# Pooling groups in reverse order, their sums on VectorE alone, values between the pooling maps, and no meeting before the prompt attention

## The reference

```python
def causal_multiscale_pool(u_hist, u_new, positions, w_pool, pool_scale):
    ...
    for g, w in enumerate(POOL_WINDOWS):
        sl = slice(g * POOL_GROUP_W, (g + 1) * POOL_GROUP_W)
        wsum = cs[:, end:end + S, sl] - cs[:, end - w:end - w + S, sl]
        count = jnp.minimum(float(w), positions + 1.0)[:, None]
        outs.append(wsum / count - uf[..., sl])
    d = jnp.stack(outs, axis=2)
    y = jnp.einsum('bsgi,gio->bsgo', d, w_pool.astype(jnp.float32)).reshape(B, S, POOL_W)
    y = y * pool_scale.astype(jnp.float32)
...
    pool_out, new_hist = causal_multiscale_pool(u_hist, u, positions, w_pool, pool_scale)
    attn_out = attend(q_nope, q_rope, lat, k_rope, w_uk, w_uv)
    x = x + gate1 * (jnp.concatenate([pool_out, attn_out], axis=-1) @ w_out)
```

## Time and profile before

| | us |
|---|---|
| runs of the kernel before (3) | 1543.78, 1548.8, 1551.41; median 1548.8 |
| the profiled execution's own time | 1546.44 |
| its span, first to last instruction | 1544.6 |
| TensorE busy in the span | 1489.1 (96%) |
| VectorE, ScalarE, GpSimd busy | 681.6, 426.7, 395.4 |

### The profile page before, as it was taken

One profiled execution on the slowest core, in us unless ns is written; L12 is line 12 of the kernel. 1 busy time (PEld: TensorE's weight loads), 2 busy tenths in 40 slices (PEclk: granted clock), 3 DMA queues, 4 the chain that ended last, 5 costly groups with the idle time before them and its releaser, 6 DMA issues.

```text
span 1544.6 us, 23703 instructions
## 1 busy us (share of the span) xinstructions
PE 1489.1 (96%) x9757; PEld 1338.5 (87%) x9757; DVE 681.6 (44%) x1464; ACT 426.7 (28%) x920; POOL 395.4 (26%) x295
## 2 busy tenths in 40 slices
PE   6899878999999999999999999999999999999998
PEld 4799766666676666689999999999999999999997
DVE  3854756566443333366663223232332323323245
ACT  4421445555433333332230110201102021020244
POOL 1232412222331111160233330604206042060400
PEclk8799999999999999999999999999999999999999
DMA  9511132332544444360012120301103021030103
GB/s 347 224 48 57 72 102 79 127 106 87 196 168 164 162 160 155 124 199 14 28 44 66 41 69 1 96 14 54 56 1 96 14 65 45 1 108 3 42 1 116
DMA packets 92442, 137.18 MB, mean 89 GB/s; under 512 B 13707, under 2 KB 64855, under 8 KB 88103
## 3 DMA queue, kind: packets, MB, share of 16 engines
q1 hardware_dynamic: 82229, 93.37, 18.5%
q0 software_dynamic: 5760, 37.75, 6.9%
q10 hardware_dynamic: 4346, 4.54, 0.9%
HBM read 121.98 MB, written 13.79 MB: 88 GB/s over the span
## 4 chain that ended last, share of the span: by engine, by line
PE 88%; DVE 5%; ACT 2%; issue 2%; DMA 2%; POOL 0%; SPq 0%; ACTq 0%; DVEq 0%
PE psa L1242 25%; PE psa L1256 24%; PE psa L1220 6%; PE psa L1092 4%; PE psa L1119 4%; PE psa L787 3%; PE psa L1159 3%; PE psa L832 3%; PE psa L955 3%; PE psa L993 3%; PE psa L1122 2%; DMA wm<-in_w_mod 2%; PE psa L976 1%; PE psa L1143 1%; PE psa L393 1%
## 5 line engine op out<-in xcount | busy, mean ns | idle before, releaser
L1242 PE MATMUL psa<-hhi,wr 128*128 128x384 f32 (+1 forms) x1536 | 374.5, 326 | 0.0
L1242 PEld LDWEIGHTS psa<-hhi,wr 128*128 128x128 f32 x1536 | 270.8, 188 | 0.1
L1256 PE MATMUL psa<-g_hi,wd_hi 128*128 128x384 f32 (+1 forms) x768 | 251.3, 327 | 0.0
L1242 PE MATMUL psa<-hlo,wr 128*128 128x384 f32 (+1 forms) x768 | 250.3, 326 | 0.0
L1256 PE MATMUL psa<-g_hi,wd_lo 128*128 128x384 f32 (+1 forms) x768 | 250.3, 326 | 0.0
L1256 PE MATMUL psa<-g_lo,wd_hi 128*128 128x384 f32 (+1 forms) x768 | 250.2, 326 | 0.0
L1673 ACT ACTIVATE g_relu<-psa 128x384 f32<-128x384 f32 (+1 forms) x96 | 45.4, 473 | 600.9 <-PE psa L1242 600.9
L2155 DVE SCALAR_TENSOR_TENSOR xT<-psa,modT,xT 128x384 f32<-128x384 f32 (+1 forms) x216 | 123.2, 571 | 189.4 <-PE psa L1256 160.6
L566 POOL TENSOR_SCALAR wr<-wraw 128x1024 fp32r<-128x1024 f32 x34 | 36.4, 1070 | 564.1 <-PE psa L1242 491.8
L2222 DVE TENSOR_TENSOR psa<-psa,g_relu 128x384 f32<-128x384 f32 (+1 forms) x96 | 52.2, 544 | 261.3 <-ACT g_relu L1673 261.3
L1242 PEld LDWEIGHTS psa<-hlo,wr 128*128 128x128 f32 x768 | 144.1, 188 | 0.1
(11 more groups left out here) (328 smaller groups left out, 2482.2 us busy)
## 6 DMA issues: line engine op xcount, KB each, us to landing
wmod<-in_w_mod SPq DMA_DIRECT2D x8, 2048.0 KB, 7.9
wraw<-in_w_up SPq DMA_DIRECT2D x32, 512.0 KB, 4.0
wraw<-in_w_down SPq DMA_DIRECT2D x32, 512.0 KB, 3.3
wm<-in_w_mod SPq DMA_DIRECT2D x4, 2048.0 KB, 20.1
x_scr<-xT SPq DMA_DIRECT2D x1, 4352.0 KB, 19.6
wraw<-in_w_out SPq DMA_DIRECT2D x8, 512.0 KB, 6.7
out_y_p<-yst SPq DMA_DIRECT2D x8, 512.0 KB, 2.6
xstage<-in_x_prompt SPq DMA_DIRECT2D x3, 1024.0 KB, 10.8
```

The source lines that it names most:

```text
L1242: mm = pe.matmul(out[:, :N], w[:, c * P:c * P + P], x[:, c, c0:c0 + N], start=(c == 0 and q == 0), stop=(c == KD - 1 and q == 2))
L1256: mm = pe.matmul(out[:, :N], w[:, c, n * P:n * P + P], x[:, c, c0:c0 + N], start=(c == 0 and q == 0), stop=(c == FG - 1 and q == 2))
```

## The change

The groups are multiplied in the order 3, 2, 1, 0 (`GROUP_ORDER`), and the weights loaded in that order. VectorE makes all four groups' sums; GpSimd's are gone, and with them the buffers `pc` and `pd`. The pooling maps run in the order of groups 1, 0, 3, 2 (`MAP_ORDER`). The first two tiles' latents are turned inside the product of the last group, and the rotary key is turned by a plain matmul into one bank's two row strips instead of by a transpose into two banks. The first query tile uses other banks. Value tiles and maps alternate, starting with a value tile; tiles 5, 6 and 7 move behind the turning of the queries and the keys. The meeting of the engines is gone; single waits take its place.

```diff
+GROUP_ORDER = (3, 2, 1, 0)
+MAP_ORDER = (1, 0, 3, 2)
+Q_BANKS = ((5, 6), (0, 1))
...
-    pa = at("pa", [P, PADL + TP], F32, R0)
+    pa = at("pa", [P, PADL + TP], F32, X0 + 20864)
...
         sp.wait_ge(sem("stored"), 16 * (2 + NB))
-        barrier(sp, 1)
+        sp.wait_ge(sem("q_mm"), TT)
+        sp.wait_ge(sem("split"), 10)
...
-        g.wait_ge(sem("u_ev"), NG)
-        g.wait_ge(sem("d_raw"), 1)
-        g.wait_ge(sem("split"), 10)
-        sums = ((pc, pc_s), (pd, pd_s))
...
-            g.tensor_tensor(a[:, first:], have[0][:, first:], have[0][:, first - s:PADL + TP - s], ALU.add)
...
-        barrier(g, 1)
...
+        def turn_rope(t):
+            n = tile_rows(t)
+            out = bank(4)[32 * (t % 2):32 * (t % 2) + DR, 0:n]
+            pe.matmul(out, krot[:n, t, :], ident[:n, :n], start=True, stop=True).then_inc(sem("turned"), 1)
...
+            if m == 3:
+                turn_latents(0)
+                turn_latents(1)
             for c in range(KD):
+                if m == 3 and c == 2:
+                    pe.wait_ge(sem("u_ev"), 3)
+                    turn_rope(0)
+                    turn_rope(1)
...
-            pe.wait_ge(sem("u_ev"), 4 if t else 3)
...
+            if t == 1:
+                pe.wait_ge(sem("u_ev"), 4)
...
-        pool_map(0)
-        for t in range(PT):
-            if t in (3, 6):
-                pool_map(t // 3)
+
+        def make_v(t):
...
-        pool_map(3)
-        barrier(pe, 1)
+
+        make_v(0)
+        for t in range(1, 5):
+            make_v(t)
+            pool_map(t - 1)
...
-            out = bank(3 - w)
+            out = bank(3 - w) if hh else bank(4 + w)
...
+            if hh == 0:
+                pe.wait_ge(sem("pool_ev"), 9)
...
         for w in range(2):
             turn_q(0, w)
+        make_v(5)
+        make_v(6)
         for m in range(2):
             make_k(m)
+        make_v(7)
         scores(0)
...
-        act.wait_ge(sem("d_raw"), 3)
+        for m in range(3):
+            u_out(m)
         turned_hi(0)
         turned_hi(1)
-        act.wait_ge(sem("u_mm"), 12)
+        u_out(3)
         pool_in_hi(0)
...
-        barrier(act, 1)
...
-        for g in range(3):
+        v.wait_ge(sem("wq_split"), 1)
+        for g in GROUP_ORDER[:3]:
             pool_raw(g)
...
         turned_lo(1)
-        pool_in_lo(0)
+        pool_raw(GROUP_ORDER[3])
...
             if t in (1, 4, 7):
-                g = t // 3 + 1
-                if g >= 2:
-                    pool_in_lo(g - 1)
+                pool_in_lo(t // 3)
...
+        values_out(0)
+        values_out(1)
+        pool_in_lo(3)
+        for t in range(2, 5):
+            values_out(t)
...
-        barrier(v, 1)
...
+        v.wait_ge(sem("lat_out"), 64)
         for w in range(2):
             q_lo(0, w)
+        values_out(5)
+        values_out(6)
         for m in range(2):
             k_lo(m)
+        values_out(7)
+        v.memset(pt0[:, 1, 0:P], 0.0)
         rope_lo(0)
```

More of the change, by code:

```diff
@@ L817, in _, with turn_latents @@
             project(t, range(KD))
+        def turn_latents(t):
+            n = tile_rows(t)
+            if t >= 2:
+                pe.wait_ge(sem("turned_lo"), t - 1)
+            pack = bank(2 + t % 2)
+            for c in range(CC):
+                pe.transpose(pack[:, c * P:c * P + n], cqn[:n, t, c * P:c * P + P], ident[:n, :n])
+                pe.transpose(pack[:, (2 + c) * P:(2 + c) * P + n], lat[:n, t, c * P:c * P + P], ident[:n, :n])
+        def turn_rope(t):
+            n = tile_rows(t)
+            out = bank(4)[32 * (t % 2):32 * (t % 2) + DR, 0:n]
+            pe.matmul(out, krot[:n, t, :], ident[:n, :n], start=True, stop=True).then_inc(sem("turned"), 1)
         for m in range(NG):
@@ L835, in _ @@
                             mm.then_inc(sem("u_mm"), 1)
-        def turn_latents(t):
-            n = tile_rows(t)
-            pe.wait_ge(sem("u_ev"), 4 if t else 3)
[L840 to L846, removed]
         def make_q(t):
@@ L869, in _ @@
                 turn_latents(t + 2)
+                turn_rope(t + 2)
         for g in range(NG):
@@ L875, in _, with pool_map @@
         mm.then_inc(sem("hist_back"), 1)
-        def pool_map(g):
-            if g == 0:
+        def pool_map(m):
+            g = MAP_ORDER[m]
+            if m == 0:
                 pe.wait_ge(sem("split"), 10)
@@ L881, in pool_map @@
                 pe.wait_ge(sem("q_ev"), TT)
-            pe.wait_ge(sem("d_lo"), g + 1)
-            if g >= 2:
-                pe.wait_ge(sem("pool_ev"), 3 * (g - 1))
+            pe.wait_ge(sem("d_lo"), m + 1)
+            if m >= 2:
+                pe.wait_ge(sem("pool_ev"), 3 * (m - 1))
             for q, (w, x) in enumerate(products(wg_hi, wg_lo, d_hi, d_lo)):
                 for b, (c0, N) in blocks():
-                    mm = pe.matmul(bank(POOL_BANKS[g % 2][b])[:, :N], w[:, 1, g * P:g * P + P], x[:, g, c0:c0 + N],
+                    mm = pe.matmul(bank(POOL_BANKS[m % 2][b])[:, :N], w[:, 1, g * P:g * P + P], x[:, g, c0:c0 + N],
                                    start=(q == 0), stop=(q == 2))
@@ L904, in _ @@
             mm.then_inc(sem("v_mm"), 1)
-        pool_map(3)
-        barrier(pe, 1)
+        make_v(0)
+        for t in range(1, 5):
+            make_v(t)
+            pool_map(t - 1)
         def turn_q(hh, w):
-            out = bank(3 - w)
+            out = bank(3 - w) if hh else bank(4 + w)
             if w == 0:
                 pe.wait_ge(sem("qh_in"), 16 * hh + 16)
+            if hh == 0:
+                pe.wait_ge(sem("pool_ev"), 9)
+            if hh == 1:
+                pe.wait_ge(sem("v_ev"), PT)
             if w == 0 and hh >= 1:
                 pe.wait_ge(sem("mod_ev"), 3 + hh)
-            if w == 1 and hh == 1:
-                pe.wait_ge(sem("q_lo"), 2)
             if w == 1 and hh >= 2:
@@ L1420, in _, with u_out @@
                     h_high(piece[0], c)
-        for m in range(NG):
+        def u_out(m):
+            g = GROUP_ORDER[m]
             act.wait_ge(sem("u_mm"), 3 * (m + 1))
@@ L1473, in _ @@
         pool_in_hi(3)
-        for g in range(NG):
-            act.wait_ge(sem("pool_mm"), g + 1)
-            if g == 2:
+        for m, g in enumerate(MAP_ORDER):
+            act.wait_ge(sem("pool_mm"), m + 1)
+            if m == 2:
                 act.wait_ge(sem("q_rotated"), TT)
@@ L1509, in first_four @@
                 act.wait_ge(sem("pt_mm"), groups_turned(i) - 1)
+                if i == 4:
+                    act.wait_ge(sem("stored"), 16 * (2 + NB))
                 if t == 4 and hh >= 1:
@@ L1972, in the_rest @@
                 v.wait_ge(sem("pv_mm"), 2 * hh - 1)
+            if i == 4:
+                v.wait_ge(sem("stored"), 16 * (2 + NB))
             if t == 4 and hh >= 1:
```

79 lines of the change are left out of this document (32 added, 47 removed).

## The result

The changed kernel takes 1532.23 us (median of 6 runs, 1530.49 to 1537.52); the kernel before, in the same comparison, 1544.62 (6 runs, 1543.24 to 1551.41). The ratio is 0.9913, 95% interval 0.9896 to 0.9929, so 11 to 16 us less. The profiled execution took 1530.49, the shortest of the six.

A forecast was written before the change was run, and what follows sets the result against it. TensorE was taken as the bound, holding 88% of the chain of waits. 12.0 us at the scores plus 1.5 for the clock gave 13.5, so 1532.9 or 1535.3 by starting figure; forecast 1534, range 1527 to 1541.

The forecast's parts named there:

- the main sum: From the pooling-input product to the prompt attention: first scores at 211.7 instead of 223.66, 12.0 us earlier.
- Sums on VectorE: Pooling-input product: VectorE makes all groups' sums, 9.7 us for window 16, each done before the next group, 12.0 apart.
- The third query tile: Query loop: tile 2 starts at 167.8, 5.1 us earlier, after a pause of 2.0 in place of 5.06, at full clock.
- The key turn: Rotary key by plain matmul: 0.27 us each against 0.11 by transpose, bounds 0.11 and 0.31; five add 0.16 each.
- Values, maps, no meeting: After the queries: value tiles cover the 2.55 pause, the meeting's 1.60 goes, keys end at 207.3 instead of 219.94.
- Scores: Start of prompt attention: VectorE's queue delays the rotary remainder; scores at 211.7, TensorE pause about 3.0.
- The clock behind it: Prompt attention: full clock rate instead of half at its start could save 0 to 3.2 us; 1.5 taken.
- the rival on it: Clock still falls before the scores: the 1.5 is gone, gain 12.0, time 1536; chance 0.28.
- The slower rival: Clock stays low through queries, values and keys after tile 2's pause; up to 1576 us; chance 0.02.
- VectorE was no bound of the later tiles: Rival, query loop: VectorE's rotation, remainders and map parts set the pace; 4.2 lost, gain 9.3, time 1538; chance 0.14.
- nothing reaches the end: Rival, after the scores: a transfer or later stage takes the lead back; time 1547.6; chance 0.04.

The follow-up runs named there:

- e1: Kernel before with GpSimd's 13 instructions for the window-16 sums left out, old order and meeting kept; 1537.22 us, ratio 0.9949 to the kernel before.
- e2: Changed kernel with GpSimd's 13 window-16 sum instructions added again, into buffers nobody reads; 1543.64 us, ratio 0.9985 to the kernel before.
- e5: Changed kernel with the rotary key of tiles 2 to 8 turned by a transpose instead of a plain product; 1532.21 us, ratio 0.9913 to the kernel before.
- e4: Changed kernel with the first pooling map put ahead of the first value tile; 1537.57 us, ratio 0.9944 to the kernel before.
- e3: Changed kernel with the meeting of the engines restored and values 5 to 7 made ahead of the last map again; 1537.77 us, ratio 0.9936.
- e6: Changed kernel with the first rotary key and query splits ahead of the key splits on ScalarE and VectorE; 1529.24 us, ratio 0.9894.
- e8: Changed kernel with both the rotary key turned by transposes and the rotary splits ahead of the key splits; 1533.55 us, ratio 0.9909.
- e9: e8 with nine more matmuls, result unused, filling TensorE's pause ahead of tile 2's queries; 1528.58 us, ratio 0.9886 to the kernel before.
- e7b: Changed kernel with 12 more matmuls, result unused, filling the pause ahead of the scores; 1534.47 us, ratio 0.9928 to the kernel before.

## Why the prediction was right, step by step

The time came out at 1532.2 for 1534, within the range, and the main sum, 12.0 us at the scores, measured 11.95. Its terms did not all do as well, and that both figures come so close is in part luck. To set the forecast's times beside the changed kernel's trace, 1.64 us are added to the latter.

*Sums on VectorE*: as forecast. The window-16 group's sums begin at 123.03 and are done at 132.5, 9.5 us for the 9.7 of the forecast, 2.4 ahead of the next group. e1 prices the other half, GpSimd's sums gone, at 7.93 us at the scores, and e2 shows the mechanism from the other side.

*The third query tile*: VectorE's part came as forecast. GpSimd's last split ended at 160.98 + 1.64 = 162.62 (forecast 162.6), and the tile begins at 167.56 (167.8). But the pause is 1.19 and not 2.0: VectorE was 0.24 sooner, and TensorE came to the pause 0.57 later than forecast (166.37 for 165.8), held up by the dearer key turns.

*The key turn*: mis-sized. In the query loop five turns take 0.86 us, of which four transposes are 0.43, so the key turn is 0.43 where I took 0.27 and had 0.31 as the upper bound; by a transpose (e5) it adds 0.03 and not the 0.11 that I set against it. So the edit cost 0.40 us a tile in place of 0.16, and seven tiles took 19.48 us and not 18.8. The Trainium skill, TensorE: Matmul & The Clock Gate, section Terms, has a transpose mode four times faster for FP32. That factor gives the loop's 0.43 (4 x 0.108), but not the other rows of plain FP32 products here. Inside the last group's product two key turns together took 0.43 us (149.56 less about 149.13, the end of the matmuls ahead of them by their spacing), and the three products of the earlier trace rows took 0.77, since the next work on TensorE's timeline of the kernel before is

```profile
18.73 2.55 PE L765 MATMUL psa<-ident,xstage 128*128 128x128 f32 x24
```

That is 0.22 and 0.26 each; my 0.31 was read from the row's length. Why a single one between transposes costs twice as much no run shows.

*Values, maps, no meeting*: as forecast, with no pause left (values straight behind the turned history, turned queries at 199.19 behind the last map). Here small errors cancelled. The queries ended 0.44 later than forecast (187.04 for 186.6); the turned history gave back 0.24 (0.79 us for 1.03), values and maps 0.10 (13.00 for 13.1), turned queries, two values and keys 0.24 (6.33 for 6.57), and 0.13 were lost again between keys and scores (4.55 for 4.42). Put back singly, the old order and the meeting cost 4.33, of which 1.7 is the clock (e4), and 2.49 (e3). All that the change brings besides e1 is 4.03 us at the scores: e1's kernel still pauses for 1.00, 0.94, 0.33, 2.54, 1.60 and 3.72 us between product and scores, 10.13 in all, the changed kernel for 1.19 and 3.03, 4.22 in all. Of the 5.91 saved, 1.9 went into TensorE's own work; the dearer key turns, seven in the loop at about 0.40, more than account for that. The reverse order of the groups and the turning inside the last product were not taken back by themselves.

*Scores*: VectorE's queue was what was late, as said: the last value's copy, a memset and the rotary remainder end it. The pause was 3.03, forecast 3.0. e6 shows that 1.95 of it was the order of that queue and of ScalarE's, since it moves the rotary splits in both.

*The clock behind it*: this step failed. I expected the pause of 3.0 to keep the clock and full rate to save 1.5. The clock fell, as in the rival on it (0.52 on the mean of 210 to 215), and the attention up to its last sixteen matmuls took 189.99 us for 189.74, so nothing was saved. What a kept clock would have brought stays open: e8, e9 and e7b kept it there and took 188.28, 190.11 and 193.28 us. By the sum less this term, 12.0 from the middle of the runs, the time is 1536; the 1532 measured is lower because the time of before in the same comparison is 1544.6 and not 1548.8, and the difference of the medians is 12.4. By the ratio the gain is 11 to 16 us, which holds 12.0 as well as 13.5, so the times do not show that the term is wrong, the trace does. And the 1.7 us that the clock gave at the last sixteen matmuls stand in no term of the forecast.

The slower rival (clock low through queries, values and keys) did not come: 1.00 in all windows from 160 to 210 us. VectorE was no bound of the later tiles: their period of 3.06 is TensorE's own, and with the shorter turns 2.63. That nothing reaches the end is out by the ratio.

## What to carry to other kernels

Before work is given to an idle GpSimd, look at what VectorE does in those microseconds: here 13 instructions cost 8 us where a map waited for their result (e1) and 10 where nobody did (e2). Read small gains from one trace, from the begin of an untouched stage to the begin of the next one, check that the times agree, and look at the clock in between. Price an operation by a row with the same neighbours, from its begin to the begin of the next, and put a clock gain into the sum as a range that reaches down to nothing.

## What the runs showed of the hardware that was not expected

- Pauses of the same length kept the clock in one kernel and lost it in another: 2.54 to 2.55 us kept it in the kernel before and in e1, lost it in e4; 1.09 to 1.10 ahead of the scores kept it in e8 and e9, lost it in e6; at the third query tile 1.19 kept it in the changed kernel, 1.80 and 1.82 lost it in e8 and e5.
- The fall that follows costs different amounts: 1.7 us behind e4's pause, 1.6 behind the one of e8 that e9 fills. The attention up to its last sixteen matmuls took 192.47 and 193.28 us with a fall of 10 to 14 us in the first head (e3, e7b), 188.28 with one of some 3.5 us (e8), and 189.2 to 190.1 in the eight others.
- Beside GpSimd even a VectorE instruction of 176 columns took 2.05 us instead of 0.33 (e2 and the changed kernel, the window-2 group's small sum): the price is the rest of GpSimd's instruction, whatever VectorE's own size, while a remainder that reads PSUM kept its 0.41.
- A plain FP32 product with 128 moving columns took 0.43 us alone between transposes, and 0.22 with a second one behind it (the changed kernel's key turns).
